# A third bank for turning the attention weights, and the scan's ignored operand moved into the bank of its own scores

## What is computed

```python
z = jnp.einsum("bhqd,bhkd->bhqk", q_blk, k_pre) * scale
strict = k_pos[None, :] < q_pos[:, None]
log_rest = jnp.where(strict, jax.nn.log_sigmoid(-z), 0.0)
suffix = lax.cumsum(log_rest, axis=3, reverse=True) - log_rest
a = jnp.where(strict, jnp.exp(jax.nn.log_sigmoid(z) + suffix), 0.0)
out = jnp.einsum("bhqk,bhkd->bhqd", a, v_pre)
```

## Time and profile before

| | us |
|---|---|
| median of 3 runs | 2045.06 |
| lowest, highest | 2044.89, 2047.67 |
| the profiled execution, its own time | 2047.72 |
| its span (first to last instruction) | 2045.9 |
| TensorE busy in it | 1976.6 (97%) |
| VectorE, ScalarE, GpSimd busy | 1333.8, 862.0, 577.2 |

### The profile page before, as it was taken

The page is one execution under the profiler, slowest core; times in us unless marked ns, Lnnn a source line. Parts: engine busy times, 40 slices in busy tenths (PEclk is TensorE's granted clock), DMA queues, the critical chain, the costliest instruction groups (busy, mean ns, idle before and its releaser), DMA issues. The chain is left out here.

```text
span 2045.9 us, 25158 instructions
## 1 busy us (share of the span) xinstructions
PE 1976.6 (97%) x9345; PEld 1627.2 (80%) x9345; DVE 1333.8 (65%) x1813; ACT 862.0 (42%) x1523; POOL 577.2 (28%) x424
## 2 busy tenths in 40 slices
PE   6999999999999899989999999999999999999997
PEld 5788888887887688766688888877788888878885
DVE  6756556559798632387655655568656556579896
ACT  6433333434445311277634444444443443434443
POOL 1345555530002122055321100221555455410000
PEclk8999999999999999999999999999999999999999
DMA  4223223235500222544134322140322322265102
GB/s 145 77 73 98 82 68 99 83 146 187 182 11 11 67 85 90 142 95 103 32 103 136 112 83 62 56 116 15 113 83 73 93 83 73 72 252 170 62 1 83
DMA packets 216466, 190.15 MB, mean 93 GB/s; under 512 B 7532, under 2 KB 171928, under 8 KB 216344
## 3 DMA queue, kind: packets, MB, share of 16 engines
q1 hardware_dynamic: 216256, 188.51, 30.0%
q10 hardware_dynamic: 88, 0.02, 0.0%
HBM read 152.85 MB, written 35.65 MB: 92 GB/s over the span
## 5 line engine op out<-in xcount | busy, mean ns | idle before, releaser
L1829 DVE TENSOR_TENSOR w_lo<-st,w_hi 128x512 fp32r<-128x512 f32 x160 | 173.5, 1086 | 178.6 <-ACT w_hi L1407 178.6
L950 PE MATMUL ps<-T_hi,w_lo 128*128 128x512 f32 x640 | 249.1, 389 | 0.3 <-issue 0.3
L951 PE MATMUL ps<-T_lo,w_hi 128*128 128x512 f32 x640 | 249.0, 389 | 0.0
L952 PE MATMUL ps<-T_hi,w_hi 128*128 128x512 f32 x640 | 249.0, 389 | 0.0
L950 PE MATMUL ps<-tr_hi,sr_lo 128*128 128x512 f32 x616 | 241.9, 393 | 5.1 <-DVE xT L2060 2.7
L952 PE MATMUL ps<-tr_hi,sr_hi 128*128 128x512 f32 x616 | 239.8, 389 | 0.0
L951 PE MATMUL ps<-tr_lo,sr_hi 128*128 128x512 f32 x616 | 239.8, 389 | 0.0
L950 PE MATMUL ps<-B_hi,w_lo 128*128 128x512 f32 x576 | 227.0, 394 | 10.9 <-DVE B_lo L1829 4.5
L951 PE MATMUL ps<-B_lo,w_hi 128*128 128x512 f32 x576 | 225.9, 392 | 0.0
L952 PE MATMUL ps<-B_hi,w_hi 128*128 128x512 f32 x576 | 225.7, 392 | 0.0
L950 PE MATMUL ps<-act_hi,wb_lo 128*128 128x512 f32 x384 | 152.3, 397 | 3.1 <-DVE wb_lo L1829 1.6
(11 more groups left out here) (257 smaller groups left out, 4220.4 us busy)
## 6 DMA issues: line engine op xcount, KB each, us to landing
gate_raw<-in_ffn_w_gate SPq DMA_DIRECT2D x44, 512.0 KB, 5.3
up_raw<-in_ffn_w_up SPq DMA_DIRECT2D x44, 512.0 KB, 5.1
h_spill<-up_s SPq DMA_DIRECT2D x66, 256.0 KB, 2.0
piece_A<-in_ffn_w_down SPq DMA_DIRECT2D x32, 512.0 KB, 4.5
piece_B<-h_spill SPq DMA_DIRECT2D x32, 512.0 KB, 6.0
wa_raw<-in_w_in SPq DMA_DIRECT2D x16, 512.0 KB, 4.0
wb_raw<-in_w_out SPq DMA_DIRECT2D x16, 512.0 KB, 3.8
wb_raw<-in_mem_w_kv SPq DMA_DIRECT2D x16, 512.0 KB, 3.8
```

The costliest lines, as they stand in the source:

```text
L950: pe.matmul(to, w_lo, m_hi, start=first, stop=False, skip_group_check=joins)
L951: pe.matmul(to, w_hi, m_lo, start=False, stop=False, skip_group_check=joins)
L952: return pe.matmul(to, w_hi, m_hi, start=False, stop=last, skip_group_check=joins)
L1829: return dve.tensor_tensor(to, value, plain(hi), ALU.subtract)
```

## The change

Bank 4 becomes a third bank for turned weights: parts use the banks 5, 6, 4 in turn, and part nth waits for part nth - 3. The scan's ignored operand is now a column of the first bank of scores of its own tile. So the scan waits until both sigmoids of the tile have read that bank, and the scores of a later tile in the same banks wait for the scan too. At the end, the first tile of the output projection waits until the last part that was turned in bank 4 has been copied out.

```diff
-        STILL_BANK = a_bank[A_PROJ + 4]
-        TURN_BANKS = [b for b in (4, 5, 6) if b != STILL_BANK]
-        assert STILL_BANK != 7
+        TURN_BANKS = (5, 6, 4)
...
-            return [(turns_before[m] + n, TURN_BANKS[(turns_before[m] + n) % 2], 4 * n, min(4 * n + 4, i + 1))
+            return [(turns_before[m] + n, TURN_BANKS[(turns_before[m] + n) % 3], 4 * n, min(4 * n + 4, i + 1))
...
                 if z_free_after[m]:
                     pe.wait_ge(s_sig, 2 * z_free_after[m])
+                    pe.wait_ge(s_scan, z_free_after[m])
...
-                    if nth >= 2:
-                        pe.wait_ge(*turned(nth - 2))
+                    if nth >= 3:
+                        pe.wait_ge(*turned(nth - 3))
...
                 if s == M + 4:
-                    pe.wait_ge(s_scan, M)
+                    pe.wait_ge(*turned(max(n for n in range(len(turn_of)) if TURN_BANKS[n % 3] == 4)))
                     tile(B_STEPS[0])
...
-                dve.wait_ge(s_sig, 2 * m + 1)
-                dve.tensor_tensor_scan(r[:, ::-1], r[:, ::-1], ps[:, STILL_BANK, 0:1].broadcast_to([P, n]), 1.0,
+                dve.wait_ge(s_sig, 2 * m + 2)
+                dve.tensor_tensor_scan(r[:, ::-1], r[:, ::-1],
+                                       ps[:, z_bank[m][0], 0:1].broadcast_to([P, n]), 1.0,
                                        ALU.mult, ALU.bypass).then_inc(s_scan, 1)
```

## The result

The changed kernel takes 2062.3 us in the median of three runs (2060.82 to 2062.4), where the kernel before took 2045.06 (2044.89 to 2047.67): ratio 1.0065, 95% interval 1.0049 to 1.0081. That is 17.2 us by the medians, and 14.6 by the two profiled executions (spans 2060.5 and 2045.9). The forecast was 12.4 more, 2057.5 us, in a range of 2050 to 2064.

The account below looks back on a forecast made before the run. TensorE, busy 97% of the span, was taken to bound the kernel, so its standstills count: first round 3.6, three rounds 8.1, end 0.7, together 12.4 us on the median 2045.06, giving 2057.5 us, range 2050 to 2064.

Parts of the forecast that it names:

- rival 3: Scans end before TensorE wants their banks, so only the third bank acts, saving 8.6 us: 2036.5 us, chance 0.04.
- rival 2: Waits are traded evenly, the longer loop showing at half the places, 0 to 4 us in all: 2047 us, chance 0.12.
- The walk of the second round: Start times followed through tiles 16 to 31: TensorE 1.7, then 2.4, then 2.7 us late per round.
- second half: Late part of a round, scan 27 to tile 29's last transposes: lateness grows from 1.7 to 2.7 us, adding 1.0.
- What was costed at nothing: The scan column's new place, GpSimd's later product and the SP queue's loads were given no cost.
- the signs named: Expected in the profile: ScalarE copy waits under 3 us, VectorE's about 10, scores waiting for scans, middle round 35.8 us.
- The first round: First of the stage's four rounds: 3.6 us late, from 2.1 at tile 5, 0.45 more, and 1.0 in its later part.
- the 0.45: In the opening round, added because tile 5's first part, then at the lower clock, is now out of the way.
- The end: The output projection waits for ScalarE's copy of the last part, number 95 in bank 4: 0.7 us.
- The clock: Three falls of TensorE's clock in the stage, about 1.6 us each, kept in the sum as before.
- Rival 1: Two falls of TensorE's clock in each round, five more than now, 8 us: 20 in all, 2065 us, chance 0.13.
- Rival 4: The third bank does nothing at all, 2 to 3 us more: 2060 us, within the range, counted in the main 0.71.

Follow-up runs that it names:

- e12: The changed kernel as it is, measured once more beside other kernels: 2062.29 us, ratio 1.0069 to the kernel before.
- e6: The changed kernel with the order of its three banks turned to 4, 5, 6: 2059.87 us, ratio 1.0061 to the kernel before.
- e7: The changed kernel with VectorE's copy of tile s - 4 ahead of its scan: 2062.78 us, ratio 1.0070 to the kernel before.
- e4: The kernel before with one wait more, scores waiting for the scan of the tile that held their banks: 2050.18 us, ratio 1.0008.
- e8: The kernel before with VectorE's copy ahead of its scan: 2044.61 us, ratio 0.9986.
- e5: The changed kernel without the third bank, both new waits kept: 2064.97 us, ratio 1.0085 to the kernel before.
- e1: The kernel before with the scan's ignored operand in SBUF in place of bank 4: 2068.09 us, ratio 1.0103.

## Why the prediction was right

**Direction and mechanism** were right: rival 3 (faster) and rival 2 (traded evenly) fail at the place that I named, scores 22, which start 0.12 us after scan 20 ends. The walk of the second round holds step by step. Scores 20 begin at 908.38 now, 4.07 us later than before (904.31); with that taken off, scores 22 are at 909.4 (forecast 909.4), scan 22 at 912.4 (912.4), scores 24 at 914.6 (914.5), scan 23 at 915.2 (915.2) and the second part of tile 21 at 918.1 (918.2). So does its second half: scan 27 at 923.1 (923.2), scores 29 at 924.4 (924.5), the last transposes of tile 29 at 935.8 (935.8). The round grew by 2.66 us for a forecast 2.7. What was costed at nothing held too: a scan over 1024 keys takes 2.29 us for 2.27 before, and no sigmoid waits for a product of GpSimd. Of the signs named, one missed: the transposes' waits for VectorE's copies grew to 7.9 us, not to about 10.

**A wait that I missed**: scores 21 need scan 19, and wait 0.48 us (909.87 above). It costs nothing, as the standstill before scores 22 is shorter by as much.

**The first round** was put at 3.6 and is 3.0, by e12 against the profiled execution of before, from the first matmul of the pool's map to the end of the last transpose of tile 13 (44.07 and 41.03 us, each with one fall of the clock). Two errors partly cancel in it. With e12's start, 0.11 us later, taken off, the second part of tile 5 goes at 885.5, which is 3.1 us later than the 882.4 of before, not 2.1. And the 0.45 added to that has the wrong sign. The fall of the trace before lasted past tile 5 (PEclk 0.67 from 883 to 886) and slowed the work there, while e12 has 1.00 in that stretch; by the scores of tile 12 the shift is down to 2.1 us (890.03 and 887.86). The second half then adds 1.0, as forecast. That the sum came out near is luck in part.

**The end** is 0.7 for 0.7, shown by e6.

**The clock** was the uncertain term. I kept three falls in the stage, as before has. The changed kernel's profile has five, one of them behind the last round, and one more in the first feed-forward part, where nothing was changed. The part from 637 to 645 us, before and after:

```profile
637.00:645.00 8.00, 5.26 (x24) 1.00 0.00 0
```

```profile
637.00:645.00 8.00, 5.27 (x17) 0.79 0.00 0
```

By the spans, then: 1.2 ahead of the stage, 2.8 for the first round, 2.7, 4.2 and 1.1 for the others, 2.4 for the end (0.7 and a fall) and 0.2 behind it, 14.6 in all. The first round has two falls here and is some 0.3 us shorter than e12's with one, so a fall doesn't cost 1.6 us everywhere. e12 has four falls in the stage and none ahead of it, and is 13.7 longer than before. Rival 1, five falls more for 8 us, did not come in full; one to three did. Without any the sum of the terms as measured is 3.0 + 3 x 2.66 + 0.7 = 11.7, for 12.4.

The Trainium skill, "TensorE: Matmul & The Clock Gate", section "A second HAM failure mode: psum-queue depth-cycling", which I weighed as a rule, tells of a kernel in which a TensorE idling between groups as it goes round its banks swings between its levels. Three of the changed kernel's four rounds are like that and the second isn't. Other runs don't settle what brings a fall. e7 has standstills of 1.8 us and no fall in rounds two to four, but is at 0.83 from 866 to 906.61 us. e4 stands still more than before, and its eleven executions have mean clocks of 0.990 to 0.994, where before's have 0.988 to 0.993 on that chip. e8, no slower than before, has the same 0.79 from 637 to 645 us as the changed kernel.

**The base** makes up the rest: the 17.2 us are against a median of three runs, 2045.06, while 23 runs of the same kernel beside e12 have theirs at 2048.95, from 2045.4 to 2053.05. Executions with the same mean clock are the fairest pair: at 0.991 and 0.992, nine of before have a median of 2047.74 and three of e12 one of 2061.16, 13.4 us apart. So the loss is 13 to 14 us by most measures, 1 to 2 more than the forecast, and the difference is of the size of a fall.

**Rival 4**, that the third bank does nothing at all, is wrong by e5: it gives 0.95 us a round.

## What to carry to other kernels

A buffer is freed by its last reader. Handing one more reader a buffer that is in a ring lengthens the ring's loop by that reader's whole time and by its queueing, and a spare buffer won elsewhere doesn't pay for that where the same engine is late in both places. Walk one steady round from the timeline, with every queue in order: it foretold single starts of the second round to 0.1 us, and missed by 1.0 us in the first, where the clock fell. And judge a change of a per cent by clean rounds, not by totals in which the clock's falls, at 1.6 us each, come and go.

## What the hardware showed that I had not expected

The ignored operand of a scan is read all the same. From SBUF it slows VectorE's scan (2.27 to 3.18 us over 1024 keys) and GpSimd's product (2.00 to 3.25 us over 1023) where the two run side by side, and e1 is 20 us slower in all, an estimated 6 of them by more falls of the clock. I had taken the still bank for a waste of PSUM.
